# The even attentions' subtraction reads the spread maxima from SBUF, copied there by ScalarE

## Chip, core and metric

One Trainium2 chip, one of its cores. The metric is the device time of one execution in microseconds. Engines are named as in the profile: PE is TensorE, DVE is VectorE, ACT is ScalarE, POOL is GpSimd. All data is 32-bit float.

## The reference, cut to what matters

The network has two blocks of a first model and one of a second. Only the first layer (the "even" one) is touched: two attentions over 1024 latent tokens and 256 context tokens, 8 query heads and 2 key heads of width 64. Attention A lets every latent query see all 1280 keys; attention B sees a band of three 128-key tiles, the context, and one extra "sink" logit.

```python
def gqa_attend(q, k, v, bias=None, sink=None):
    s = jnp.einsum("bqhgd,bkhd->bhgqk", q, k) * ATTN_SCALE
    if bias is not None:
        s = s + bias
    ...
        p = jax.nn.softmax(s, axis=-1)
    return jnp.einsum("bhgqk,bkhd->bqhgd", p, v)
```

The softmax is computed with a maximum that is subtracted before the exponential. The sum of the exponentials divides the result at the end.

## The kernel before

Scores are held transposed: 128 keys on the partitions, and 8 heads x 128 queries along a row, so one **item** is one key tile of one query tile, 128x1024 numbers. A **group** is one query tile with all its key tiles: in A eight groups of 10 items and two context groups of 2 (84 items), in B groups of 4 or 5 and two of 2 (42 items). The functions `soft_attention` of PE, ACT and DVE and `prob_sums` of POOL run A, then B; between them the projections of B are computed, and nothing else overlaps them.

`group_plan` writes the order out by hand as steps, one item per step. Every engine goes through the same steps in program order, so an engine that waits holds back all its later work:

- F, "fill": PE computes the scores of item n into one of two PSUM buffers (L1056), and ACT copies them into an SBUF ring (L1569). DVE keeps a running maximum over the items of the group, reading the PSUM scores and the SBUF maximum (L2046, `maximum`).
- M0, M1, R0, R1: after the group's last item PE transposes the maximum (L1043) and DVE reduces it over the keys, negated (L2072); in B the sink is taken in (L2079, L2080), which are two instructions on 8 columns.
- NB: PE spreads the 8 negated maxima over 128 partitions and 1024 columns with 8 transposes into two PSUM banks, `NM_BC` (L1068).
- B: three steps after the group's last fill and later, one item per step: DVE adds `NM_BC` to the item in the ring (L2029, `subtract`), ACT takes the exponential in place (L1578), POOL adds the item to the group's running sum of probabilities (L650; none for the first item of a group, as the second add takes both), and two steps later PE multiplies with the values (L1089).
- OE, DEN, RC, MIX, OM: at the end of the group the output is gated (L2053), PE turns the sums into denominators (L1108), DVE takes reciprocals (L2065 in A, L2063 in B), PE spreads them (L1100), and DVE multiplies them in (L2087).

The ring has 17 items in A and 12 in B; a fill waits until the item that lay in its place has been multiplied and added. DVE's order in a step is: closing work of an older group, `subtract`, `maximum`; only in the NB step does the maximum go first. ACT's order is fill, then exponential. PE's NB waits until the negated maxima are ready and until DVE has subtracted the last item of the group before, since `NM_BC` has one copy:

```python
pe.wait_ge(at["neg_max"], g + 1)
if g:
    pe.wait_ge(at["shifted"], first[g])
```

Of the kernel before, what the change touches and what calls it, by code (L numbers as in the profile page):

```python
# [6 lines left out]
ACT = mybir.ActivationFunctionType  # L7
# [3 lines left out]
P = 128  # L11
# [120 lines left out]
def program(nc, wall, wdown, wglr, wgate2, vec, xl_in, xc_in, consts, ropes, bmask, dmask, rpb, out):  # L132
    with ExitStack() as ctx:
# [248 lines left out]

        scale_q = DH ** -0.5

        MASK_PREV, MASK_NEXT = area(SCR + 6656, P), area(SCR + 6656 + P, P)
        LOW = [XL[:, k, :] for k in range(KT)] + [area(SCR + 1024 * i, 1024) for i in range(6)]
        HIGH = [area(22016 + 4 * TOK + 1024 * i, 1024) for i in range(5)]
        XC_LOW, XC_HIGH = XC[:, 0:1024], XC[:, 1024:2048]
# [14 lines left out]
        for name, groups, ring, g_rows in (("A", [group_a(*x) for x in lat_ctx], LOW + HIGH, 0),  # L403
                                           ("B", [group_b(*x) for x in lat_ctx], LOW, 4)):
            items, first, plan = group_plan([len(gr["keys"]) for gr in groups])
            at = {"groups": groups, "items": items, "first": first, "plan": plan, "ring": ring[:-2], "sums": [XC_HIGH, ring[-1]],
                  "maxes": [XC_LOW, ring[-2]], "g_rows": g_rows,
                  "sink": name == "B"}
            for x in ("st", "filled", "masked", "maxed", "max_t", "reduced", "neg_max", "bcast", "shifted", "exped", "pooled",
                      "pv", "o_out", "den", "recip", "r_bcast", "mixed") + (("sink_in", "sink_out") if name == "B" else ()):  # L410
                at[x] = sem(f"att{name}_{x}")
            at["is_masked"] = [groups[g]["keys"][j][1] is not None for g, j in items]
            at["max_before"] = [first[g] - g for g in range(len(groups) + 1)]
            at["misc"] = []
            for st in plan:
                for half in range(2):
                    at["misc"] += [("MT", st[f"M{half}"], half)] if f"M{half}" in st else []
                at["misc"] += [("MIX", st["MIX"], 0)] if "MIX" in st else []
                at["misc"] += [("DEN", st["DEN"], 0)] if "DEN" in st else []
            soft[name] = at  # L420
# [349 lines left out]
        def _(pe):  # L770
# [258 lines left out]
            def soft_attention(at, t_next):  # L1029
# [31 lines left out]
                for st, ahead in zip(at["plan"], at["plan"][1:] + [{}]):  # L1061
                    if "NB" in st:
                        g = st["NB"]
                        pe.wait_ge(at["neg_max"], g + 1)
                        if g:
                            pe.wait_ge(at["shifted"], first[g])
                        for h in range(HEADS):
                            mm = pe.transpose(ps[:, NM_BC + h * P:NM_BC + (h + 1) * P],  # L1068
                                              ST[:, g % 4, 1, h:h + 1].to_broadcast([P, P]), IDENT)
                        mm.then_inc(at["bcast"], 1)  # L1070
                    if "F" in ahead:
                        fill(ahead["F"])
                    for half in range(2):
                        if f"M{half}" in st:
                            max_transposes(st[f"M{half}"], half)
                    if "PV" in st:
                        n = st["PV"]
                        g, j = items[n]
                        kt = groups[g]["keys"][j][0]
                        pe.wait_ge(at["exped"], n + 1)  # L1080
                        if j == 0 and g:
                            pe.wait_ge(at["o_out"], g)
                        p = ring[n % len(ring)]
                        for kv in range(2):
                            for half in range(2):
                                r = slice(64 * half, 64 * half + 64)
                                o = PV_O + 256 * kv
                                heads = p[:, kv * BANK:(kv + 1) * BANK].rearrange("p (x a q) -> p x a q", x=2, a=2)[:, :, half, :]
                                mm = pe.matmul(ps[r, o:o + 256], VE[:, kt, 64 * kv:64 * kv + 64], heads,  # L1089
                                               start=(j == 0 and kv == 0), stop=(j == len(groups[g]["keys"]) - 1),  # L1090
                                               skip_group_check=True)
                        mm.then_inc(at["pv"], 1)
                    if "MIX" in st:
                        g = st["MIX"]
                        pe.wait_ge(at["recip"], g + 1)
                        misc_wait("MIX", g, 0)
                        for x in range(4):
                            for half in range(2):
                                h = 2 * x + half
                                mm = pe.matmul(ps[64 * half:64 * half + 64, MISC + x * P:MISC + (x + 1) * P],  # L1100
                                               ST[:, g % 4, 2, h:h + 1].to_broadcast([P, 64]), IDENT, start=True, stop=True)
                        mm.then_inc(at["r_bcast"], 1)
                    if "DEN" in st:
                        g = st["DEN"]
                        pe.wait_ge(at["pooled"], at["max_before"][g + 1])
                        misc_wait("DEN", g, 0)
                        for h in range(HEADS):
                            mm = pe.matmul(ps[:, MISC + 2 * h:MISC + 2 * h + 2], at["sums"][g % 2][:, h * P:(h + 1) * P], ONES[:, 0:2],  # L1108
                                           start=True, stop=True)
                        mm.then_inc(at["den"], 1)  # L1110
# [329 lines left out]
        def _(act):  # L1440
# [115 lines left out]
            def soft_attention(at):  # L1556
                ring, items = at["ring"], at["items"]
                for st in at["plan"]:
                    if "F" in st:
                        n = st["F"]  # L1560
                        if at["is_masked"][n]:
                            act.wait_ge(at["masked"], sum(at["is_masked"][:n + 1]))
                        else:
                            act.wait_ge(at["st"], n + 1)
                        if n >= len(ring):
                            act.wait_ge(at["pv"], n - len(ring) + 1)
                            act.wait_ge(at["pooled"], pooled_upto(at, n - len(ring)))
                        o = S_T + 2 * (n % 2) * BANK
                        act.activation(ring[n % len(ring)], ps[:, o:o + 2 * BANK], ACT.Copy).then_inc(at["filled"], 1)  # L1569
                    if at["sink"] and "NB" in st:  # L1570
                        g = st["NB"]
                        act.wait_ge(at["sink_in"], g + 1)
# [180 lines left out]
        def _(dve):  # L1753
# [264 lines left out]
            def soft_attention(at):  # L2018
# [5 lines left out]
                def subtract(n):  # L2024
                    g, j = items[n]
                    if j == 0:
                        dve.wait_ge(at["bcast"], g + 1)
                    p = ring[n % len(ring)]
                    dve.tensor_tensor(p, ps[:, NM_BC:NM_BC + 1024], p, ALU.add).then_inc(at["shifted"], 1)  # L2029

                def maximum(n):
                    g, j = items[n]
# [455 lines left out]
```

## Time and profile before

| | us |
|---|---|
| median of 3 runs | 3201.89 (3201.58 to 3202.61) |
| the profiled execution, its own time | 3198.09 |
| its span in the trace | 3196.3 |
| PE busy | 3028.5 (95%) |
| DVE busy | 1480.0 (46%) |
| ACT busy | 761.3 (24%) |
| POOL busy | 596.5 (19%) |
| POOL's adds of probabilities, L650, 106 of them | 251.0 |
| DVE's subtractions, L2029, 126 of them | 151.4 |

The busy shares are those of the whole program, most of which is matrix products; what counts here are the two attentions, from 247.8 us (the first ACT fill) to about 530 us, and from about 712 us to about 916 us. POOL works in them far more than its 19% says. The last two rows are sums of the groups of the page by line.

### The profile page before, as it was taken

What the parts mean: (1) busy time and instruction counts of PE and PEld (TensorE: products, weight loads), DVE (VectorE), ACT (ScalarE), POOL (GpSimd) and SP (SyncE); (2) the same over time, 40 slices, a digit from 0 to 9 for tenths busy, and PEclk for the clock granted to TensorE, in tenths of its full rate; (3) what the DMA queues carried; (4) which work ended last, traced back from release to release, by engine and by line L of the source; (5) the groups of instructions that cost most, each with busy time, mean ns of one, the idle gap of its engine ahead of it and who ended that gap; (6) DMA issues with size and microseconds to landing.
All of it is one profiled execution on the core that took longest, in us unless ns stands there. A gap on an engine that the chain in (4) does not pass through costs nothing.

```text
span 3196.3 us, 27666 instructions
## 1 busy us (share of the span) xinstructions
PE 3028.5 (95%) x11326; PEld 1554.0 (49%) x11326; DVE 1480.0 (46%) x1858; ACT 761.3 (24%) x923; POOL 596.5 (19%) x394
## 2 busy tenths in 40 slices
PE   7998898997889999999999999999999999999997
PEld 4563445653455545444774545454444444444443
DVE  4636873248846586735773311035453343340001
ACT  4116662005410210113641122122012222220000
POOL 0004673003410122233441000000112222210000
PEclk9999998999889899999999899999999999999998
DMA  6001000020033211123221001100211111112101
GB/s 222 27 27 40 1 1 7 27 87 1 1 121 110 112 40 40 40 68 80 55 91 45 30 20 40 33 27 20 92 40 43 50 40 41 52 50 89 36 36 53
DMA packets 41071, 162.42 MB, mean 51 GB/s; under 512 B 5265, under 2 KB 5777, under 8 KB 36721
## 3 DMA queue, kind: packets, MB, share of 16 engines
q1 hardware_dynamic: 34704, 143.18, 12.8%
q0 software_dynamic: 6240, 17.47, 2.2%
q8 instruction: 90, 1.47, 0.2%
q14 instruction: 37, 0.30, 0.0%
HBM read 148.04 MB, written 15.20 MB: 51 GB/s over the span
## 4 chain that ended last, share of the span: by engine, by line
PE 86%; DVE 7%; ACT 3%; issue 2%; POOL 1%; DMA 1%; SPq 0%; DVEq 0%; ACTq 0%; POOLq 0%
PE ps L794 28%; PE ps L787 20%; PE ps L1433 9%; PE ps L1319 4%; PE ps L1272 3%; PE ps L1206 2%; PE ps L1056 2%; PE ps L969 2%; PE ps L1089 2%; PE ps L984 2%; PE ps L998 2%; PE ps L1108 1%; PE ps L902 1%; DVE x_ctx L2046 1%; DVE arena L2046 1%
## 5 line engine op out<-in xcount | busy, mean ns | idle before, releaser
L787 PE MATMUL ps<-arena 128*128 128x512 f32 (+1 forms) x1632 | 625.6, 544 | 15.8 <-ACT arena L1485 10.9
L787 PEld LDWEIGHTS ps<-arena 128*128 128x128 f32 x1632 | 311.5, 192 | 321.0 <-issue 306.8
L794 PE MATMUL ps<-arena 128*128 128x512 f32 x936 | 411.3, 592 | 3.2 <-DVE arena L2248 1.6
L794 PE MATMUL ps<-x_lat,arena 128*128 128x512 f32 x688 | 303.9, 592 | 0.0
L794 PEld LDWEIGHTS ps<-arena 128*128 128x128 f32 x936 | 177.6, 190 | 227.2 <-issue 223.8
L1433 PE MATMUL ps<-arena 128*128 128x512 f32 x616 | 264.5, 592 | 0.0
L794 PEld LDWEIGHTS ps<-x_lat,arena 128*128 128x128 f32 x688 | 130.7, 190 | 164.5 <-issue 164.5
L1056 PE MATMUL ps<-arena 64*128 64x512 f32 x504 | 152.7, 687 | 49.6 <-DVE x_ctx L2046 23.8
L1433 PEld LDWEIGHTS ps<-arena 128*128 128x128 f32 x616 | 117.0, 190 | 147.3 <-issue 147.3
L2223 DVE SCALAR_TENSOR_TENSOR x_ctx<-arena,vectors,x_ctx 128x1024 f32<-128x1024 f32 x120 | 169.6, 1413 | 3.5
L1468 ACT ACTIVATE arena<-x_lat 128x1024 f32<-128x1024 f32 x40 | 42.0, 1050 | 465.7 <-DVEq L2177 343.3
L794 PE MATMUL ps<-x_lat,x_ctx 128*128 128x512 f32 x336 | 147.6, 592 | 0.0
L2169 DVE TENSOR_TENSOR x_lat<-ps,x_lat 128x1024 f32<-128x1024 f32 x10 | 12.2, 1224 | 279.1 <-PE ps L1433 279.0
L1319 PE MATMUL ps<-arena 128*128 128x512 f32 x256 | 123.7, 606 | 0.0
L2383 DVE TENSOR_TENSOR x_ctx<-ps,x_ctx 128x512 f32<-128x512 f32 x21 | 14.5, 692 | 225.9 <-ACT x_ctx L1742 225.9
L725 POOL TENSOR_TENSOR arena<-arena 128x512 f32<-128x512 f32 x6 | 10.8, 1793 | 580.3 <-DMA arena<-in_wall 449.1
L794 PEld LDWEIGHTS ps<-x_lat,x_ctx 128*128 128x128 f32 x336 | 63.8, 190 | 80.4 <-issue 80.4
L1056 PEld LDWEIGHTS ps<-arena 64*128 64x128 f32 x504 | 40.7, 196 | 104.2 <-DVE x_ctx L2046 43.3
L1906 DVE SCALAR_TENSOR_TENSOR arena<-arena,silu_c 128x128 f32<-128x128 f32 (+1 forms) x224 | 89.9, 479 | 0.0
L1578 ACT ACTIVATE x_lat<-x_lat 128x1024 f32<-128x1024 f32 x70 | 73.8, 1055 | 65.4 <-DVE x_lat L2029 64.5
L1272 PE MATMUL ps<-arena 128*128 128x512 f32 x192 | 85.4, 604 | 1.8 <-DMA arena<-in_wall 1.8
L2029 DVE TENSOR_TENSOR x_lat<-ps,x_lat 128x1024 f32<-128x1024 f32 x70 | 84.2, 1212 | 2.4 <-PE ps L1068 2.1
(284 smaller groups left out, 4137.3 us busy)
## 6 DMA issues: line engine op xcount, KB each, us to landing
arena<-in_wall SPq DMA_DIRECT2D x188, 512.0 KB, 3.8
arena<-in_wdown SPq DMA_DIRECT2D x7, 1408.0 KB, 6.0
x_lat<-in_xl_in SPq DMA_DIRECT2D x8, 1024.0 KB, 9.5
residual_store<-x_lat SPq DMA_DIRECT2D x8, 1024.0 KB, 6.8
x_lat<-residual_store SPq DMA_DIRECT2D x8, 1024.0 KB, 8.6
x_lat<-expanded_bias POOLq DMA_DIRECT2D x48, 160.0 KB, 3.6
arena<-expanded_bias POOLq DMA_DIRECT2D x32, 160.0 KB, 4.0
out<-x_lat SPq DMA_DIRECT2D x8, 512.0 KB, 3.0
```

The source lines that it names most:

```text
L787: mm = pe.matmul(ps[:, o + c:o + c + n], W[:, ring_of(g) % WSLOTS, k, :], rhs(k, c, n), start=(k == 0), stop=(k == KT - 1))
L794: mm = pe.matmul(ps[:, bank * BANK:(bank + 1) * BANK], weights[:, k, :], tokens[:, k, :], start=(start and k == 0), stop=(k == 3), skip_gr ...
L969: mm = pe.matmul(ps[:, o:o + n], DQ[r, j, qt * P:(qt + 1) * P], DK[r, j, k0:k0 + n], start=True, stop=True)
L984: mm = pe.transpose(ps[:, o:o + P], DP[u % 3][:, a, i * P:(i + 1) * P], IDENT)
L1056: mm = pe.matmul(ps[:, o:o + BANK], QK[r, 4, kt * P:(kt + 1) * P], QK[r, 0:4, c0:c1], start=True, stop=True)
L1272: mm = pe.matmul(ps[:, o:o + 512], HG[:, k, i * P:(i + 1) * P], W[:, :, k, :], start=(k == 0), stop=(k == KT - 1))
L1319: mm = pe.matmul(ps[:, R_PS + c:R_PS + c + n], W[:, (g0 + 16 + m) % WSLOTS, k, :], HG[:, k, c:c + n], start=(k == 0), stop=(k == KT - 1))
L1433: mm = pe.matmul(ps[:, o + c:o + c + n], wd[:, k, :], ACTV[:, k, c:c + n], start=(k == 0), stop=(k == DOWN_K - 1))
L1578: act.activation(p, p, ACT.Exp).then_inc(at["exped"], 1)
L1906: ins = dve.scalar_tensor_tensor(t, x, SC[:, k, a:a + 1], t, ALU.mult, ALU.add)
L2029: dve.tensor_tensor(p, ps[:, NM_BC:NM_BC + 1024], p, ALU.add).then_inc(at["shifted"], 1)
L2223: link(dve.scalar_tensor_tensor(acc, U[:, j, k:k + LAT], V[:, w + k:w + k + 1], acc, ALU.mult, ALU.add))
```

## The change

The 8 transposes of NB still go to PSUM. Then ACT copies the two banks into a new SBUF tile `NMS` of 1024 columns, and DVE's subtraction reads `NMS` where it read PSUM. There are 20 such copies, one for each group. PE's next NB waits for the copy (`spread`) and no longer for the last subtraction; the copy takes over that wait, because `NMS` has one copy too. The two 128-column masks of B move 512 columns up to make room.

```diff
-        MASK_PREV, MASK_NEXT = area(SCR + 6656, P), area(SCR + 6656 + P, P)
+        NMS = area(SCR + 6 * 1024, 1024)
+        MASK_PREV, MASK_NEXT = area(SCR + 7 * 1024, P), area(SCR + 7 * 1024 + P, P)
...
                         pe.wait_ge(at["neg_max"], g + 1)
                         if g:
-                            pe.wait_ge(at["shifted"], first[g])
+                            pe.wait_ge(at["spread"], g)
...
                         act.activation(ring[n % len(ring)], ps[:, o:o + 2 * BANK], ACT.Copy).then_inc(at["filled"], 1)
+                    if "NB" in st:
+                        g = st["NB"]
+                        act.wait_ge(at["bcast"], g + 1)
+                        if g:
+                            act.wait_ge(at["shifted"], at["first"][g])
+                        act.activation(NMS, ps[:, NM_BC:NM_BC + 1024], ACT.Copy).then_inc(at["spread"], 1)
...
                     if j == 0:
-                        dve.wait_ge(at["bcast"], g + 1)
+                        dve.wait_ge(at["spread"], g + 1)
                     p = ring[n % len(ring)]
-                    dve.tensor_tensor(p, ps[:, NM_BC:NM_BC + 1024], p, ALU.add).then_inc(at["shifted"], 1)
+                    dve.tensor_tensor(p, NMS, p, ALU.add).then_inc(at["shifted"], 1)
```

On ACT, in attention A, around the NB step of the fifth group, the order before is (L1569 the fill, L1578 the exponential):

```order
L1569 ACTIVATE x_lat<-ps 128x1024 [waits attA_pooled,attA_pv,attA_st]
L1578 ACTIVATE x_lat<-x_lat 128x1024 [waits attA_shifted]
L1569 ACTIVATE x_lat<-ps 128x1024 [waits attA_pooled,attA_pv,attA_st]
L1578 ACTIVATE x_lat<-x_lat 128x1024 [waits attA_shifted]
L1569 ACTIVATE x_lat<-ps 128x1024 [waits attA_pooled,attA_pv,attA_st]
```

and in the changed kernel, at the same place (L1570 the fill, L1576 the copy, L1585 the exponential):

```order
L1570 ACTIVATE x_lat<-ps 128x1024 [waits attA_pooled,attA_pv,attA_st]
L1585 ACTIVATE x_lat<-x_lat 128x1024 [waits attA_shifted]
L1570 ACTIVATE x_lat<-ps 128x1024 [waits attA_pooled,attA_pv,attA_st]
L1576 ACTIVATE arena<-ps 128x1024 [waits attA_shifted,attA_bcast]
L1585 ACTIVATE x_lat<-x_lat 128x1024 [waits attA_shifted]
L1570 ACTIVATE x_lat<-ps 128x1024 [waits attA_pooled,attA_pv,attA_st]
```

The copy stands between the fill and the exponential of the NB step. On DVE, around the NB step of the second group of A, the order before is (L2029 the subtraction, L2046 the maximum, L2053 the gating of OE):

```order
L2029 TENSOR_TENSOR arena<-ps,arena 128x1024
L2046 TENSOR_TENSOR x_ctx<-ps,x_ctx 128x1024 [waits attA_maxed,attA_filled] x2
L2029 TENSOR_TENSOR arena<-ps,arena 128x1024 [waits attA_bcast]
L2029 TENSOR_TENSOR arena<-ps,arena 128x1024
L2046 TENSOR_TENSOR x_ctx<-ps,x_ctx 128x1024 [waits attA_maxed,attA_filled]
L2053 TENSOR_TENSOR arena<-ps,arena 128x4x128 [waits attA_pv]
```

and in the changed kernel, where the three are L2036, L2053 and L2060:

```order
L2036 TENSOR_TENSOR arena<-arena 128x1024
L2053 TENSOR_TENSOR x_ctx<-ps,x_ctx 128x1024 [waits attA_maxed,attA_filled] x2
L2036 TENSOR_TENSOR arena<-arena 128x1024 [waits attA_spread]
L2036 TENSOR_TENSOR arena<-arena 128x1024
L2053 TENSOR_TENSOR x_ctx<-ps,x_ctx 128x1024 [waits attA_maxed,attA_filled]
L2060 TENSOR_TENSOR arena<-ps,arena 128x4x128 [waits attA_pv]
```

No instruction of DVE moves. Both inputs of the subtraction are now in SBUF (`arena`), and the first one of a group waits for the copy in place of the transposes.

## Rows read from the trace of the kernel before

**Rows 1.** Stages: span; PE, PEld, DVE, ACT, POOL busy (instructions); PE clock; DMA.

```profile
272.00:504.00 232.00, 206.39 (x1300) 98.43 (x1300) 189.86 (x187) 151.05 (x154) 171.19 (x72) 0.95 0.05 12
504.00:529.00 25.00, 18.86 (x112) 15.89 (x112) 4.05 (x9) 1.33 (x2) 7.62 (x4) 0.58 0.00 1
734.00:893.00 159.00, 131.33 (x824) 70.43 (x820) 131.76 (x145) 75.50 (x86) 73.13 (x31) 0.90 0.00 1
```

**Rows 2.** Groups by line and form: busy us, mean ns, idle before.

```profile
L2029 DVE TENSOR_TENSOR arena<-ps,arena 128x1024 f32<-128x1024 f32 x56 | 67.2, 1211 | 2.7 <-PE ps L1068 2.5
L1920 DVE TENSOR_TENSOR arena<-arena 128x1024 f32<-128x1024 f32 x10 | 12.3, 1226 | 0.3
L650 POOL TENSOR_TENSOR arena<-arena,x_lat 128x1024 f32<-128x1024 f32 x31 | 73.3, 2363 | 35.4 <-ACT x_lat L1578 33.1
```

**Rows 3.** What L1068, the spreading transposes, waited for: us, times.

```profile
  DVE x_lat L2029: 4.3, 4
  DVE arena L2029: 2.2, 3
```

**Rows 4.** Timeline of DVE in another stage: start us, us, engine, line.

```profile
1107.51 2.29 DVE L1795 TENSOR_TENSOR x_lat<-arena,x_lat 128x2048 f32<-128x2048 f32 x1
1109.84 3.24 DVE L1797 TENSOR_TENSOR x_lat<-arena,x_lat 128x2048 f32<-128x2048 f32 x1
1113.01 3.35 DVE L1798 TENSOR_TENSOR x_lat<-arena 128x2048 f32<-128x2048 f32 x1
```

**Rows 5.** Timeline of POOL in the same stretch.

```profile
1107.87 3.06 POOL L702 TENSOR_TENSOR arena<-arena 128x512 f32<-128x512 f32 x1 [190.08 <-DMA arena<-in_wall]
1110.90 3.31 POOL L703 TENSOR_TENSOR arena<-arena 128x512 f32<-128x512 f32 x1
...
1117.56 1.26 POOL L709 TENSOR_TENSOR arena<-arena 128x512 f32<-128x512 f32 x1
```

**Rows 6.** L2079 in B: duration ns min/median/max, first and last start; then one timeline row.

```profile
L2079 DVE TENSOR_TENSOR softmax_stats<-softmax_stats,negated_sink x10: 166/1970/2173, 729.5 to 878.1; 128x8 f32<-128x8 f32 x10
...
781.93 2.17 DVE L2079 TENSOR_TENSOR softmax_stats<-softmax_stats,negated_sink 128x8 f32<-128x8 f32 x1
```

**Rows 7.** Timeline of POOL at that place.

```profile
781.73 2.34 POOL L650 TENSOR_TENSOR x_ctx<-x_ctx,x_lat 128x1024 f32<-128x1024 f32 x1
```

**Rows 8.** Timeline of DVE in a middle group of attention A.

```profile
360.50 2.34 DVE L2029 TENSOR_TENSOR arena<-ps,arena 128x1024 f32<-128x1024 f32 x2
...
367.75 1.21 DVE L2029 TENSOR_TENSOR arena<-ps,arena 128x1024 f32<-128x1024 f32 x1
...
370.02 1.21 DVE L2029 TENSOR_TENSOR x_lat<-ps,x_lat 128x1024 f32<-128x1024 f32 x1
...
376.34 1.23 DVE L2046 TENSOR_TENSOR x_ctx<-ps,x_ctx 128x1024 f32<-128x1024 f32 x1 [0.51 <-ACT arena L1569]
379.24 0.69 DVE L2087 TENSOR_TENSOR arena<-ps,arena 128x512 f32<-128x512 f32 x1 [1.68 <-PE ps L1100]
```

**Rows 9.** Timeline of POOL in the same group.

```profile
358.50 2.38 POOL L650 TENSOR_TENSOR x_ctx<-x_ctx,arena 128x1024 f32<-128x1024 f32 x1 [0.23 <-ACT arena L1578]
...
367.87 2.37 POOL L650 TENSOR_TENSOR arena<-arena 128x1024 f32<-128x1024 f32 x1 [0.77 <-ACT arena L1578]
```

**Rows 10.** Timeline of ACT at that group's NB step.

```profile
358.32 1.00 ACT L1569 ACTIVATE arena<-ps 128x1024 f32<-128x1024 f32 x1
```

**Rows 11.** The chain that ended last, at the end of attention A.

```profile
487.15 2.37 POOL arena L650
...
504.72 2.35 POOL arena L650
...
507.12 2.87 PE ps L1108 x16
```

**Rows 12.** Timeline of DVE at the end of attention A.

```profile
486.62 3.48 DVE L2029 TENSOR_TENSOR x_lat<-ps,x_lat 128x1024 f32<-128x1024 f32 x3
...
501.96 2.36 DVE L2029 TENSOR_TENSOR arena<-ps,arena 128x1024 f32<-128x1024 f32 x2 [0.64 <-PE ps L1068]
```

More of the change, by code:

```diff
@@ L408, in program @@
                   "sink": name == "B"}
-            for x in ("st", "filled", "masked", "maxed", "max_t", "reduced", "neg_max", "bcast", "shifted", "exped", "pooled",
+            for x in ("st", "filled", "masked", "maxed", "max_t", "reduced", "neg_max", "bcast", "spread", "shifted", "exped", "pooled",
                       "pv", "o_out", "den", "recip", "r_bcast", "mixed") + (("sink_in", "sink_out") if name == "B" else ()):
```

## The prediction

> **What bounds the kernel now.** I read the page first and then the busy times by stage, since the change touches only the two attentions. The page says that PE is 95% busy, but that is the whole program. In attention A, the first row of [rows 1], PE is busy 206 of 232 us, DVE 190, POOL 171, ACT 151, for 84 items, or 2.76 us an item. No engine is far from the bound, and all walk through the same steps in order, so what delays one delays the rest soon after. In B, its third row, DVE is busy 132 of 159 us and POOL only 73. Nothing runs beside the attentions that could fill a gap, so time lost there is time of the kernel. In the steady middle of a group of A the beat is set by DVE: two subtractions start at 367.75 and 370.02, 2.27 us apart [rows 8], which is one subtraction and one maximum with no idle between. POOL's adds last 2.36 us each [rows 2], nine to a group of ten items, and lie beside DVE's work without touching it: the subtraction with one PSUM input has a mean of 1.21 us [rows 2], though an add runs beside most of them.
>
> **What is removed.** PE's wait for the last subtraction before it spreads the next maxima. The transposes waited for it 7 times, 6.5 us in all [rows 3]. The copy takes over that wait, so where PE waited before, ACT waits now and then copies. A fill of the same size out of PSUM takes 1.00 us [rows 10]; the 8 transposes, which now run ahead of the wait, took about as long. That is an exchange, and I count nothing for it; at best 6.5 us come back.
>
> **What is added: 20 copies on ACT.** 20 x 1.00 = 20 us of ACT. At the NB step the copy stands behind the fill. The fill of [rows 10] ends at 359.32; DVE then does the maximum over it, and begins the first subtraction at 360.50 [rows 8]. A copy from 359.32 to 360.32 is ready 0.2 us before that. The exponential behind it waits for that subtraction anyway. So the copy is covered by the maximum: 0 us; if that cover is gone everywhere, 20 us. I take 0, as the one place is typical of all groups that still have fills, and the last groups have the exchange above.
>
> **What is moved: the subtraction's first input, from PSUM to SBUF.** Its own length does not change by much. DVE's addition of two SBUF inputs, L1920, has 1.226 us against 1.211 us for L2029 [rows 2]: 126 x 0.015 = 2 us, within the rest. The page "VectorE: DVE Perf Modes" of the Trainium skill, in its section on the SBUF-source errata, gives 58 cycles of fixed cost from SBUF and 120 from PSUM at 0.96 GHz, which would make it an estimated 8 us gain; the two rows here show no such difference.
>
> But with both inputs in SBUF, DVE's instruction and POOL's add are no longer independent. The trace shows it elsewhere. At 1107.51 DVE begins an addition of two SBUF inputs, which lasts its 2.29 us [rows 4]. POOL's addition begins at 1107.87 and takes 3.06 us [rows 5], where the same shape alone takes 1.26 (its last row). It ends at 1110.93, 1.13 us after DVE's end. The next of DVE began at 1109.84 and takes 3.24 us, 0.95 more than the first: it ends at 1113.08, 2.15 us after POOL's end. POOL's next, in turn, takes 3.31. They go strictly one after the other, each waiting for the whole of the other. The same thing is seen with the very add of this stage: in B the 8-column L2079, two SBUF inputs, takes 0.17 us at the least and 2.17 at the most, 1.97 in the middle [rows 6]. The one at 781.93 ends at 784.10, just after the add that ran from 781.73 to 784.07 [rows 7]. So the hold is not a matter of size, and L2029 escaped it only through its PSUM input. This is the decisive row.
>
> From those rows the holds are: DVE 2.15 us for 2048 columns, so 1.08 for 1024; POOL 1.13 for an addition that lasts 1.26, 0.13 less, so 2.36 - 0.13 = 2.23 for ours. The page "SBUF — State Buffer" of the Trainium skill, section "Who interferes with whom", states the rule: a VectorE instruction with two SBUF inputs and a GpSimd one that reads SBUF share a read interface, which the first holds for its whole instruction. It speaks against this change, and the trace agrees. With whole instructions as holds (1.22 and 2.36) in place of those measured from end to end, the lower bound below would be 84 x 1.22 + 72 x 2.36 - 232 = 40 us and not 20.
>
> **The lower bound.** From 272 to 504 us A has 84 subtractions and 72 adds [rows 1]. In turn they need 84 x 1.08 + 72 x 2.23 = 251 us, 19 more than the 232 there are. Only if neither ever left the other an unused moment would it stay at that: +19.
>
> **The upper bound.** A beat of subtraction, add, subtraction is 1.08 + 2.23 = 3.31 us where it was 2.27, so 1.04 more for each add, 74 in A: +77. In B, POOL is busy 73 of 159 us, 46%; 42 subtractions that fall in at random would wait 42 x 0.46 x 2.23 / 2 = 22 us. Together +99.
>
> **What I take.** I walk through a middle group of A. Its first subtraction at 360.50 would meet the add that began at 358.50 and ended at 360.88 [rows 8, 9]; as that add has itself been held up by the subtraction before, the wait is nearer 1.3 us than 0.4. In the steady part each subtraction starts inside an add: that of 370.02 inside the add of 367.87, which ends at 370.24 [rows 8, 9]; once POOL is behind, it waits for most of one, 1.04 per item. Of the group's other eight items some two stand where the subtractions are over 3 us apart, with reductions between them, so six count: 6.2 us. Against it, DVE has 0.51 + 1.68 = 2.2 us of idle at the group's end, waiting for PE [rows 8], which is then late no more. 1.3 + 6.2 - 2.2 = 5.3, say 5 us a group, and seven groups up to 487 us: 35 us.
>
> At the end of A the chain is POOL itself: eight adds back to back from 487.15 to 507.07, and PE's denominators wait for the last of them [rows 11]. Ten subtractions start in that time, the first as one of the three from 486.62 on, the last as one of the two from 501.96 [rows 12]. Each now takes its turn: 10 x 1.08 = 11 us, say 10 of them on the chain.
>
> In B, L2079 already waits out the running add just before the late subtractions, and L2079's own wait only grows by what POOL has been pushed. I take 8 us, between 0 and 22, nearer the lower end because POOL idles over half of B.
>
> Sum: 35 + 10 + 8 = 53 us. What is late next is PE: with more idle time its granted clock may fall. It is 0.95 in A, 0.90 in B and 0.58 in the thin end of A [rows 1]; full level is 2.4 GHz and the lower one 1.2. I put nothing into the sum for it, and some into the range. The profiled execution took 3198.1 us, so 3251 by its own time; the median of the runs is 3.8 us above it, so 3255.
>
> **The rivals.**
> 1. *The add and the subtraction do not exclude each other.* Then only the removed wait and the 2 us of the longer form count: between 3201.9 - 6.5 = 3195 and 3204. For it: the subtraction waits nowhere now. Against it: [rows 4 to 6], with half of the ten L2079 at 1.97 us or more. It would have to be that a PSUM-free subtraction is exempt. 6%, half of it faster by more than the 0.2%, about 6 us, that a measurement of this kernel can tell from no change.
> 2. *They do, but the waits hide,* because the order of the two settles so that a subtraction falls into POOL's pauses. A pause exists: POOL idles 61 of the 232 us of A. But the bound of 19 us is made without any loss, so this gives 3202 + 19 = 3221, slower all the same: 15%, in 3216 to 3230.
> 3. *ACT's copy is uncovered.* When DVE waits for POOL the copy has more time, not less, so it would take an NB step at which the fill comes late and no maximum follows. +20 on top of the forecast: 3275. 5%.
> 4. *PE's clock decides.* If A fell from 0.95 to the 0.81 or less of a stretch like its end, 206 us of PE work would become 206 x 0.95 / 0.81 = 242, +36, of which half may hide behind DVE's and POOL's waits: 3255 + 18 = 3273, and with the upper bound 3301 and more. 9%, half of it above 3300.
>
> **How the numbers follow.** The forecast, 3230 to 3300 around 3255, has 65%; rival 2 15%, rival 3 5%, rival 4 9%, rival 1 6%. The range 3216 to 3300 leaves out rival 1 and half of rival 4 and a rest at both edges, some 15% together. Faster by over 0.2%: 3%. Within 0.2%: 4%, the other half of rival 1 and a bound that was too high. Slower: 93%.
>
> **What the changed profile would show.** In A the subtraction's mean rises from 1.21 to about 1.8 us and more, with a spread from 1.2 to 3.4; the add's mean rises from 2.36 to about 3 us. The steady beat of subtractions becomes 3.3 us. The stage from 272 to 504 grows by 35 to 45 us; B's by under 20. The maximum L2046, which keeps a PSUM input, stays at 1.22 us, and projections, the odd layer and the second model keep their times. I am wrong if the subtraction keeps 1.22 us while POOL adds; the size is wrong if the adds' mean grows but the stage does not, which would mean PE set the pace after all.

## The result, and the profile after

The changed kernel takes 3253.3 us (median of 4 runs, 3251.3 to 3256.6), the kernel before 3201.7 beside it (4 runs). The ratio is 1.016, 95% interval 1.015 to 1.018: some 52 us slower. The profiled execution took 3251.3 us, its span is 3249.5.

The busy times by stage, first of the kernel before, then of the changed one. The stages are cut at the first ACT fill and the last multiplication (L2087, now L2094) of each attention: attention A, the projections between, attention B, the rest. The columns are those of [rows 1].

```profile
247.80:529.20 281.40, 242.79 (x1484) 119.92 (x1480) 209.80 (x208) 167.66 (x169) 178.80 (x75) 0.92 0.04 11
529.20:716.50 187.30, 183.43 (x630) 108.41 (x632) 61.53 (x167) 12.44 (x11) 0.00 (x0) 0.97 0.14 46
716.50:917.50 201.00, 159.88 (x980) 89.67 (x976) 148.77 (x168) 85.42 (x95) 75.47 (x32) 0.86 0.02 6
917.50:3196.30 2278.80, 2218.07 (x7330) 1103.96 (x7330) 946.40 (x1247) 438.83 (x579) 342.03 (x283) 0.98 0.17 56
```

```profile
249.00:583.20 334.20, 259.32 (x1484) 125.94 (x1481) 286.08 (x208) 176.91 (x179) 224.63 (x75) 0.87 0.03 9
583.20:767.20 184.00, 180.04 (x630) 105.51 (x632) 61.71 (x168) 12.45 (x11) 0.00 (x0) 0.99 0.14 47
767.20:966.90 199.70, 154.83 (x980) 86.22 (x976) 150.34 (x168) 94.54 (x105) 79.48 (x32) 0.89 0.02 6
966.90:3249.50 2282.60, 2221.58 (x7330) 1106.73 (x7330) 946.87 (x1246) 439.11 (x579) 341.41 (x283) 0.98 0.17 56
```

Attention A grew by 52.8 us. B did not grow at all: -1.3. The other two stages moved by -3.3 and +3.8, with the same instructions in them; by so much a stage can move with nothing changed in it. In A DVE is busy for 76 us more (same 208 instructions) and POOL for 46 us more (same 75). An instruction that waits inside the engine counts as busy, so the wait shows as duration. The subtraction and the add in the changed kernel, answering to [rows 2]:

```profile
L2036 DVE TENSOR_TENSOR x_lat<-arena,x_lat 128x1024 f32<-128x1024 f32 x70 | 131.2, 1884 | 3.4 <-ACT arena L1576 3.2
L2036 DVE TENSOR_TENSOR arena<-arena 128x1024 f32<-128x1024 f32 x56 | 111.4, 2000 | 7.3 <-ACT arena L1576 7.2
L651 POOL TENSOR_TENSOR arena<-arena,x_lat 128x1024 f32<-128x1024 f32 x31 | 89.6, 2890 | 28.1 <-ACT x_lat L1585 24.9
```

The subtraction's mean is 1.93 us (131.2 + 111.4 = 242.6 us for 126) where it was 1.21; the add's, in the form shown, 2.89 where it was 2.36. The steady part of a group, DVE's timeline in the changed kernel, answering to [rows 8], with subtraction L2036 and maximum L2053:

```profile
286.24 2.25 DVE L2036 TENSOR_TENSOR x_lat<-arena,x_lat 128x1024 f32<-128x1024 f32 x1
288.42 1.21 DVE L2053 TENSOR_TENSOR arena<-ps,arena 128x1024 f32<-128x1024 f32 x1
289.55 2.26 DVE L2036 TENSOR_TENSOR x_lat<-arena,x_lat 128x1024 f32<-128x1024 f32 x1
291.73 1.21 DVE L2053 TENSOR_TENSOR arena<-ps,arena 128x1024 f32<-128x1024 f32 x1
292.87 2.25 DVE L2036 TENSOR_TENSOR x_lat<-arena,x_lat 128x1024 f32<-128x1024 f32 x1
```

and POOL's timeline there:

```profile
284.09 9.94 POOL L651 TENSOR_TENSOR x_ctx<-x_ctx,x_lat 128x1024 f32<-128x1024 f32 x3 [2.26 <-ACT x_lat L1585]
```

The subtractions start every 3.31 us, three adds take 9.94, also 3.31 each; the maximum with its PSUM input still takes 1.21. That is the beat of the prediction to the hundredth: 1.08 + 2.23.

### The profile page after: what moved, and what is told of

It reads as the page before. It is cut to its first block, busy times and chain, and to the rows that moved or that the text cites. A ratio compares the mean times of both kernels' runs of the same rounds, so it can differ in the third digit from the quotient of the medians.

```text
span 3249.5 us, 27704 instructions
## 1 busy us (share of the span) xinstructions
PE 3041.5 (94%) x11326; PEld 1556.9 (48%) x11326; DVE 1558.6 (48%) x1858; ACT 780.0 (24%) x943; POOL 645.7 (20%) x394
## 4 chain that ended last, share of the span: by engine, by line
PE 81%; DVE 11%; issue 3%; ACT 3%; DMA 1%; POOL 0%; SPq 0%; DVEq 0%; ACTq 0%
PE ps L795 28%; PE ps L788 19%; PE ps L1434 9%; PE ps L1320 3%; PE ps L1273 3%; DVE x_lat L2036 2%; DVE arena L2036 2%; PE ps L1207 2%; PE ps L970 2%; PE ps L985 2%; DVE arena L2053 2%; PE ps L999 2%; DVE x_ctx L2053 1%; PE ps L819 1%; PE ps L903 1%
## 5 line engine op out<-in xcount | busy, mean ns | idle before, releaser
L795 PE MATMUL ps<-arena 128*128 128x512 f32 x936 | 411.3, 592 | 3.2 <-DVE arena L2255 1.6
L1434 PE MATMUL ps<-arena 128*128 128x512 f32 x616 | 264.5, 592 | 0.0
L2176 DVE TENSOR_TENSOR x_lat<-ps,x_lat 128x1024 f32<-128x1024 f32 x10 | 12.2, 1224 | 279.1 <-PE ps L1434 279.0
L2036 DVE TENSOR_TENSOR x_lat<-arena,x_lat 128x1024 f32<-128x1024 f32 x70 | 131.2, 1884 | 3.4 <-ACT arena L1576 3.2
L1320 PE MATMUL ps<-arena 128*128 128x512 f32 x256 | 123.8, 606 | 0.0
L2036 DVE TENSOR_TENSOR arena<-arena 128x1024 f32<-128x1024 f32 x56 | 111.4, 2000 | 7.3 <-ACT arena L1576 7.2
L1585 ACT ACTIVATE x_lat<-x_lat 128x1024 f32<-128x1024 f32 x70 | 73.9, 1056 | 89.8 <-DVE x_lat L2036 89.5
L651 POOL TENSOR_TENSOR arena<-arena,x_lat 128x1024 f32<-128x1024 f32 x31 | 89.6, 2890 | 28.1 <-ACT x_lat L1585 24.9
```

The costliest lines, as they stand in the source:

```text
L651: pool.tensor_tensor(total, one, ring[n % len(ring)], ALU.add).then_inc(at["pooled"], 1)
L795: mm = pe.matmul(ps[:, bank * BANK:(bank + 1) * BANK], weights[:, k, :], tokens[:, k, :], start=(start and k == 0), stop=(k == 3), skip_gr ...
L1320: mm = pe.matmul(ps[:, R_PS + c:R_PS + c + n], W[:, (g0 + 16 + m) % WSLOTS, k, :], HG[:, k, c:c + n], start=(k == 0), stop=(k == KT - 1))
L1434: mm = pe.matmul(ps[:, o + c:o + c + n], wd[:, k, :], ACTV[:, k, c:c + n], start=(k == 0), stop=(k == DOWN_K - 1))
L1585: act.activation(p, p, ACT.Exp).then_inc(at["exped"], 1)
L2036: dve.tensor_tensor(p, NMS, p, ALU.add).then_inc(at["shifted"], 1)
```

## The experiments

Each kernel ran beside the kernel before on the same chip; before had 3199.4 us there in four of the experiments (copy kept, inputs swapped, and the two without POOL's reading; 15 runs) and, on another chip, 3200.4 in the next four (half the add, B alone, the sink's minimum, the changed kernel again; 21 runs). The last two experiments ran once each, beside one run of the kernel before (3197.5).

**The copy without the new operand.** Only the subtraction's source is put back.

```diff
-                    dve.tensor_tensor(p, NMS, p, ALU.add).then_inc(at["shifted"], 1)
+                    dve.tensor_tensor(p, ps[:, NM_BC:NM_BC + 1024], p, ALU.add).then_inc(at["shifted"], 1)
...
                             pe.wait_ge(at["spread"], g)
+                            pe.wait_ge(at["shifted"], first[g])
```

> The changed kernel with one part undone: ACT still makes the 20 copies and DVE still waits for them, but the subtraction reads the spread maxima from PSUM again; PE waits for both the copy and the last subtraction. Theory (DVE's subtraction with two SBUF inputs and POOL's add exclude each other): the subtraction's mean is back at 1.21 us and the add's at 2.36, and the time at 3202, within 4 us. Rival (the copy and its waits on ACT cost the time): the time stays near 3253 and the subtraction's mean is irrelevant.

Measured: 3199.8 us (10 runs), ratio 1.0003, interval 0.9994 to 1.0013. The subtraction is back at 1.21 us, as the rows by line say (duration ns min/median/max, first and last start):

```profile
L2037 DVE TENSOR_TENSOR x_lat<-ps,x_lat x70: 1169/1214/1225, 272.1 to 888.7; 128x1024 f32<-128x1024 f32 x70
L2037 DVE TENSOR_TENSOR arena<-ps,arena x56: 1169/1214/1225, 292.4 to 870.4; 128x1024 f32<-128x1024 f32 x56
```

So the 20 copies, 20 us of ACT, and their waits cost nothing that can be measured as long as the subtraction reads PSUM, and the loss hangs on one operand of the subtraction.

**The inputs in the other order.**

```diff
-                    dve.tensor_tensor(p, NMS, p, ALU.add).then_inc(at["shifted"], 1)
+                    dve.tensor_tensor(p, p, NMS, ALU.add).then_inc(at["shifted"], 1)
```

> The changed kernel with the subtraction's two inputs in the other order (item first, spread maxima second). Theory (any two SBUF inputs exclude POOL's add): 3253 within 3 us, the subtraction's mean again near 1.94 us. Rival (only the tensor in the second place counts, or the two reads of the new 1024 columns conflict with something): the time moves by more than 10 us.

Measured: a median of 3261.9 us, with the profiled execution at 3250.2 and the three others from 3260.2 to 3267.8. In the profiled execution the subtractions are those of the changed kernel (medians 1.53 and 2.15 us, against 1.53 and 2.14), so the order plays no part in the exclusion. The median lies 9 us above the 3253 expected. To see whether that is the order's doing, the changed kernel was run again:

> The changed kernel once more, to stand beside e2_inputs_swapped, whose profiled run had 3250.2 us as the changed kernel's 3251.3, but whose timed runs lay at 3260 to 3268. If those were a drift of TensorE's granted clock on that chip (0.956 to 0.960 in them, 0.963 in the profiled run), this kernel too shows runs between 3250 and 3268. If the order of inputs costs 8 us, it stays at 3251 to 3257.

Measured: 3252.0, 3255.9, 3263.0 and 3261.4 us, at a mean PE clock of 0.962, 0.962, 0.957 and 0.959. The changed kernel spreads in the same way, and its long runs too have the lower clock. As it ran on another chip, the medians (1.019 and 1.018 of the kernel before) show only that no cost of the order can be told from this spread. The change's cost was 52 us in the first comparison and is 58 in this one. Whether the lower clock makes the long runs long, or goes with something else that does, these times do not show.

**POOL's reading taken away.** In the changed kernel and in the one before, the add becomes a fill, which takes 0.95 us.

```diff
-                    pool.tensor_tensor(total, one, ring[n % len(ring)], ALU.add).then_inc(at["pooled"], 1)
+                    pool.memset(total, 1.0).then_inc(at["pooled"], 1)
```

> The changed kernel with POOL's add of probabilities replaced by a fill of the running sum with ones, which reads nothing from SBUF; the sums of probabilities, and so the division, are left out of the computation. Theory (POOL's reading excludes DVE's two-input instruction): every subtraction takes 1.22 us, the 8-column minimum of attention B 0.17, and the time equals that of the kernel before with the same replacement, or is up to 6.5 us below it. Rival (the cost sits in the longer reading of SBUF, or in POOL's writing): the time stays some 50 us above the kernel before with the same replacement.

> The kernel before with POOL's add replaced by the same fill with ones (the sums of probabilities are left out). Theory: the 8-column minimum of attention B no longer waits (0.17 us each, 1.7 in all, where it was 16.1 us), and POOL no longer sets the end of attention A (eight adds in a row, 20 us, against ten subtractions): 3202 - 14 for the minimum - about 5 at the end of A = 3183, between 3175 and 3195. Rival (POOL costs nothing in the kernel before, as its subtraction has only one SBUF input): 3202 within 4 us.

Measured: 3185.7 us (ratio to before 0.9962, 0.9949 to 0.9975) and 3186.0 us (0.9960, 0.9945 to 0.9974), five runs each. Without reads by POOL the two kernels are equal; the change's own effect, less the exclusion, is nothing. The changed kernel's subtraction and 8-column minimum:

```profile
L2036 DVE TENSOR_TENSOR x_lat<-arena,x_lat x70: 1170/1214/1226, 273.8 to 878.7; 128x1024 f32<-128x1024 f32 x70
...
L2086 DVE TENSOR_TENSOR softmax_stats<-softmax_stats,negated_sink x10: 166/167/168, 726.3 to 866.3; 128x8 f32<-128x8 f32 x10
```

Every one of them has its plain duration. The fill also writes 1024 columns of SBUF, so it is POOL's reading, or the length of its instruction, and not its writing that holds DVE up; the length is settled by the next experiment, where an add of 1.26 us, hardly longer than the fill of 0.95, still takes turns with the subtraction. The kernel before gained 13 us by the same edit, where 14 + 5 = 19 were expected, though inside the expected range. In its profiled execution B is 12.1 us shorter (188.9, where it was 201.0), and A as a whole 2.0 (279.4, where it was 281.4), not the 5 expected of its end.

**Half the add.** POOL adds 512 columns of each item.

```diff
-                    pool.tensor_tensor(total, one, ring[n % len(ring)], ALU.add).then_inc(at["pooled"], 1)
+                    pool.tensor_tensor(total[:, 0:512], one[:, 0:512], ring[n % len(ring)][:, 0:512], ALU.add).then_inc(at["pooled"], 1)
```

> The changed kernel with POOL adding only 512 of the 1024 columns of each item (the sums of the last four heads are left out; PE takes the first four heads' twice). Theory (exclusion with holds in proportion to the instruction): the add holds 1.13 us, so subtraction, add, subtraction needs 1.08 + 1.13 = 2.21 us, below the 2.27 of DVE's own beat; the steady beat returns to 2.27 to 2.5 and the time falls to 3190 to 3205. Rival (every meeting costs a fixed time, whatever the add's length): some 50 us stay, 3235 or more.

Measured: 3203.8 us (11 runs), ratio 1.0010, 1.0001 to 1.0019, inside the range expected. The instructions still exclude each other: DVE's timeline there, and POOL's,

```profile
286.26 1.21 DVE L2036 TENSOR_TENSOR x_lat<-arena,x_lat 128x1024 f32<-128x1024 f32 x1
287.39 1.21 DVE L2053 TENSOR_TENSOR arena<-ps,arena 128x1024 f32<-128x1024 f32 x1
288.52 1.21 DVE L2036 TENSOR_TENSOR x_lat<-arena,x_lat 128x1024 f32<-128x1024 f32 x1
```

```profile
281.94 13.70 POOL L651 TENSOR_TENSOR x_ctx<-x_ctx,x_lat 128x512 f32<-128x512 f32 x6
```

The beat is 2.26 us again, and six adds of 1.26 us take 13.7, that is 2.28 each: POOL waits out every subtraction and fits into the time of the maximum. In the steady part, then, what costs is not the meeting but the sum of the two holds being longer than DVE's own beat.

That the whole time is back at that of the kernel before is partly a coincidence. Attention A and attention B of this run:

```profile
249.80:541.30 291.50, 249.19 (x1484) 122.70 (x1480) 221.73 (x208) 176.64 (x179) 132.72 (x75) 0.90 0.04 10
726.20:917.50 191.30, 155.67 (x980) 88.64 (x977) 136.48 (x168) 95.12 (x105) 44.08 (x32) 0.87 0.02 7
```

A still takes 10 us more than before (291.5, where it was 281.4) and 12 more than with POOL's reading gone (279.5); B takes 10 less, as the adds there are halved too and the sink's minimum hardly waits (0.42 us in the middle, where it was 1.97). So half the add removes some 43 of A's 53 us. Of the 10 us that stay, 8 lie behind A's sixth closing multiplication (67.3 us, where it was 59.4). There subtractions follow each other without a maximum between, and three in a row take 6.1 us, where they took 3.5. The kernel before with half the adds was not run.

**The new operand in B alone.** A reads PSUM as before, B reads the copy.

```diff
-                    dve.tensor_tensor(p, NMS, p, ALU.add).then_inc(at["shifted"], 1)
+                    dve.tensor_tensor(p, NMS if at["sink"] else ps[:, NM_BC:NM_BC + 1024], p, ALU.add).then_inc(at["shifted"], 1)
...
                             pe.wait_ge(at["spread"], g)
+                            if not at["sink"]:
+                                pe.wait_ge(at["shifted"], first[g])
```

> The changed kernel with attention A's subtraction reading PSUM again (its copies stay), so that only B's 42 subtractions read SBUF. The changed kernel's trace shows B as long as before, 199.7 us where it was 201.0, since the 8-column minimum lost 11 of the 16 us that it waited while the subtractions gained 13. Theory (the waits in B only change their place): 3197 to 3202, no difference from the kernel before that can be measured. Rival (B's share is the 8 us of the prediction): 3207.

Measured: 3201.5 us (11 runs), ratio 1.0001, 0.9992 to 1.0010. With the new operand in B alone nothing is lost that can be measured, so the 52 us are A's. The rows of B say why, two of this kernel by line (busy us, mean ns), against a minimum of 16.1 us in ten and subtractions of 1.21 us in the kernel before:

```profile
L2038 DVE TENSOR_TENSOR x_lat<-arena,x_lat 128x1024 f32<-128x1024 f32 x30 | 46.8, 1568 | 3.2 <-ACT arena L1578 3.2
...
L2088 DVE TENSOR_TENSOR softmax_stats<-softmax_stats,negated_sink 128x8 f32<-128x8 f32 x10 | 3.3, 328 | 0.3
```

**The sink's minimum out of POOL's way.** This is the kernel before, without the change. The reduction writes its 4 columns to PSUM, and what follows has one input there.

```diff
+                        if at["sink"]:
+                            c = slice(4 * half, 4 * half + 4)
+                            top = ps[:, MISC:MISC + 4]
+                            link(dve.tensor_reduce(top, ps[:, MISC:MISC + BANK].rearrange("p (h k) -> p h k", h=4), AX_X, ALU.max,
+                                                   negate=True))
+                            link(dve.tensor_tensor(nm[:, c], top, NSINK[:, c], ALU.min))
+                            if half == 1:
+                                dve.engine_nop().then_inc(at["neg_max"], 1)
+                            link(dve.tensor_tensor(top, top, vcol("sink", 4 * half, 4), ALU.add))
+                            ins = dve.tensor_scalar(ST[:, g % 4, 3, c], top, 0.0, None, ALU.min)
...
```

> The kernel before, with the sink's part in attention B in another form: the reduction writes its 4 columns to PSUM, and the minimum with the negated sink, and the sum with it, take that PSUM input and one SBUF input, half by half; two more reductions' worth of small instructions for each group, each about 0.2 us with its link. Theory (DVE's instructions with at most one SBUF input never wait for POOL): no small instruction lasts over 0.2 us, where L2079 lasted 16.1 us in ten; against it stand some 0.8 us more of small instructions in each of ten groups: 16 - 1.7 - 8 = 6 us faster, 3193. Rival (the small instructions wait for something else, or the group's pace is set elsewhere): 3199 or slower.

Measured: 3190.9 us (5 runs), ratio 0.9969, 0.9956 to 0.9981: 6 to 14 us faster than the kernel before, the fastest full kernel of this study. Its small instructions, by line:

```profile
L2080 DVE TENSOR_TENSOR ps<-ps,vectors 128x4 f32<-128x4 f32 x20 | 3.4, 169 | 0.8
L2077 DVE TENSOR_TENSOR softmax_stats<-ps,negated_sink 128x4 f32<-128x4 f32 x20 | 3.2, 162 | 0.7
L2081 DVE TENSOR_SCALAR softmax_stats<-ps 128x4 f32<-128x4 f32 x20 | 3.2, 162 | 0.7
```

9.8 us of sixty instructions stand where 16.1 + 1.7 us of twenty stood, and the longest of the sixty takes 0.17 us. Attention B is 195.0 us there, against 201.0; A, in which nothing was changed, is 2.4 us shorter in the same execution, so the 6 us of B are known to some 2 us only:

```profile
710.90:905.90 195.00, 157.13 (x980) 88.41 (x977) 140.73 (x208) 86.31 (x95) 75.56 (x32) 0.87 0.02 6
```

**The long one at the start.** In the changed kernel one subtraction, the third of A, lasts 5.2 us, more than any add. DVE's and POOL's timelines there:

```profile
277.70 5.22 DVE L2036 TENSOR_TENSOR x_lat<-arena,x_lat 128x1024 f32<-128x1024 f32 x1
```

```profile
275.93 3.43 POOL L635 DMA_DIRECT2D expanded_bias<-in_rpb  x1 [275.49 <-ACT x_lat L1585]
279.36 2.47 POOL L651 TENSOR_TENSOR x_ctx<-x_lat 128x1024 f32<-128x1024 f32 x1
```

It starts 1.66 us before the add does, and yet ends behind it, at 282.92. It is no accident of one execution: with the inputs swapped, and in the second trace of the changed kernel, it takes 5.21 us. Two kernels, one run each:

```diff
-            pool.dma_start(expanded.rearrange("h r q k -> (h r) q k"), src).then_inc(table_in, 16)
...
             prob_sums(soft["A"])
+            pool.dma_start(expanded.rearrange("h r q k -> (h r) q k"), src).then_inc(table_in, 16)
```

> The changed kernel with POOL's one DMA at the start of attention A (the expanded bias table, 3.4 us of descriptors on POOL) issued after A's adds. In the changed kernel the third subtraction of A begins at 277.70 us inside that issue and lasts 5.2 us, through the issue and the whole add behind it. Theory (it waits because of what POOL does there): the third subtraction lasts at most 2.3 us, and attention A from its first fill to its last multiplication is 2 to 4 us shorter than 334.2. Rival (the long one has another cause): it stays at about 5 us.

```diff
             pool.dma_start(expanded.rearrange("h r q k -> (h r) q k"), src).then_inc(table_in, 16)
+            pool.wait_ge(soft["A"]["exped"], 2)
+            pool.memset(XC_HIGH[:, 0:8], 0.0).then_inc(u_zero, 1)
+            pool.wait_ge(u_zero, 1)
```

> The changed kernel with a fill of 8 columns, which reads nothing, between that DMA and the first add, and a wait of POOL for it. With POOL's add replaced by a fill (e3) the third subtraction lasted 1.2 us beside the same DMA issue. Theory (an add that stands ready behind the issue takes the shared read side before it starts): the third subtraction lasts at most 2.3 us. Rival (it is the issue itself that is held together with an add somewhere behind it): it lasts about 5 us.

Measured, with the DMA moved away: the third subtraction lasts 3.34 us, above the 2.3 that I had written, since it met the add at its very start and waited for all of it (2.23 + 1.08 = 3.31). With the fill between, DVE's and POOL's timelines:

```profile
278.82 1.22 DVE L2039 TENSOR_TENSOR x_lat<-arena,x_lat 128x1024 f32<-128x1024 f32 x1
```

```profile
277.05 3.43 POOL L635 DMA_DIRECT2D expanded_bias<-in_rpb  x1 [276.61 <-ACT x_lat L1588]
280.37 0.23 POOL L637 MEMSET x_ctx<- 128x8 f32 x1
280.68 2.35 POOL L654 TENSOR_TENSOR x_ctx<-x_lat 128x1024 f32<-128x1024 f32 x1
```

Beside the same DMA issue the third subtraction takes its plain 1.22 us. So the issue itself does not hold it; an add that stands ready behind the issue does, before its own record begins. A as a whole hardly gained: from the first fill to the last multiplication 333.5 and 334.1 us, against 334.2, less than the 2 to 4 expected of the first. Up to the first closing multiplication they were 2.5 and 2.8 us shorter; they lost it again in the five groups behind it (173.3 and 174.1 us, against 171.5), at a PE clock of 0.86 in A, where the changed kernel had 0.87.

The two executions took 3260.7 and 3262.7 us, as long as the longest of the changed kernel, and their traces are the only ones of such an execution. The extra is in B, which has the same instructions as in the changed kernel. The first of the two:

```profile
765.90:974.30 208.40, 163.68 (x980) 91.65 (x976) 150.83 (x168) 94.78 (x105) 79.53 (x32) 0.84 0.02 6
```

B takes 208.4 us in both, where the changed kernel had 199.7, at a PE clock of 0.84 and 0.83 against 0.89, with DVE busy as long as there. Why is open.

## Why the prediction was right, and where it was not

**The mechanism** was right, and so was its price. The exclusion was read from [rows 4 to 7], and the beat of 3.31 us from their ends. The first and third experiments leave no other cause: put the operand back, or take POOL's reading away, and the loss is gone. The signs named came true as well: the subtraction's mean is 1.93 us, its longest 3.37 apart from the one of 5.2, and the maximum stays at 1.21 to 1.23.

**The copy at nothing** was right for the copies alone, with which the time did not move. In the groups that still have fills their cover was as described. At the end of A and B, where no maximum follows, DVE waits 10.4 us for them in the changed kernel (3.2 + 7.2 in the rows by line above), where PE waited 6.5 us for DVE [rows 3] and DVE in turn some 5 us for PE: the exchange that was counted at nothing. At the end of A it is not quite nothing once DVE is behind: two of these waits lie on the chain shown further down.

**The longer form of the instruction**: a median of 1.21 us with either source once POOL's reads are gone. The estimated 8 us gain from the page "VectorE: DVE Perf Modes" of the Trainium skill, section on the SBUF-source errata, did not come: without the exclusion the two kernels stand at 3185.7 and 3186.0.

**Attention A: 45 us forecast, 52.8 measured.** The rows of the first and sixth closing multiplication, before

```profile
319.94 0.69 DVE L2087 TENSOR_TENSOR arena<-ps,arena 128x512 f32<-128x512 f32 x1 [2.56 <-PE ps L1100]
469.79 0.69 DVE L2087 TENSOR_TENSOR arena<-ps,arena 128x512 f32<-128x512 f32 x1 [2.77 <-PE ps L1100]
```

and after,

```profile
331.18 0.69 DVE L2094 TENSOR_TENSOR arena<-ps,arena 128x512 f32<-128x512 f32 x1 [0.54 <-PE ps L1101]
502.70 0.68 DVE L2094 TENSOR_TENSOR arena<-ps,arena 128x512 f32<-128x512 f32 x1
```

give 149.9 and 171.5 us for five middle groups, 4.3 us more for each; 5 was forecast. The waits for PE of 2.6 to 2.8 us ahead of the multiplication, which the walk let absorb 2.2 us a group, are indeed down to 0.5 and none. From A's first fill to the first of these rows A lost 10.0 us where 5 were counted. The 5.2 us subtraction lies there, 4 us over its plain length; with the DMA moved away this stretch took 79.6 us and with the fill between 79.3, where it was 82.2, so it accounts for half of the 5 us that were not counted. Where the other half lies was not tried. The larger miss is the end: from 469.79 to the last multiplication A took 59.4 us before and 80.5 after, 21 us more, where the forecast had one group and the end, 15. The failed step there is "the chain is POOL itself": the eight adds took 26.0 us where they had taken 19.9, 6 us more and not the 10 counted, but they no longer end last. The chain is now DVE's, and then the copies':

```profile
524.48 3.52 DVE x_lat L2036 x2
...
528.90 3.37 DVE x_lat L2036
...
532.39 3.17 DVE arena L2036
...
536.16 9.29 DVE arena L2036 x3
...
546.44 1.02 ACT arena L1576
...
547.48 4.56 DVE arena L2036 x2
...
553.03 1.01 ACT arena L1576
...
554.07 3.75 DVE arena L2036 x2
```

Where [rows 11] have eight adds back to back, the five subtractions from 528.90 on each start inside an add with no maximum before them to use the time, and last 3.1 to 3.4 us. The walk put ten subtraction holds on POOL's chain, and left out that DVE, too, loses the whole add each time. Behind them come the last two groups, each of which must wait for the exponential of the group before and for its copy: 2.0 us twice, half of it the copy (1.02 and 1.01). From the end of the eighth add, at 550.95, PE's denominators come 9.6 us later, where they followed in 0.05 us before.

**Attention B: +8 forecast, -1.3 measured.** The step that failed is "L2079's own wait only grows by what POOL has been pushed". The subtractions of B did gain 13.4 us (42 of them, 64.0 where 50.6 stood), between the 8 taken and the 22 of the upper bound. But the minimum, L2079 and now L2086, fell from 16.1 us to 4.9. In [rows 6, 7] it started 0.20 us inside the second add of its group and waited it out. In the changed kernel that add, pushed back by a subtraction, starts 0.20 us behind the minimum, and the next subtraction meets it instead (two lines of DVE, one of POOL):

```profile
835.07 0.17 DVE L2086 TENSOR_TENSOR softmax_stats<-softmax_stats,negated_sink 128x8 f32<-128x8 f32 x1
836.50 2.24 DVE L2036 TENSOR_TENSOR x_lat<-arena,x_lat 128x1024 f32<-128x1024 f32 x1
```

```profile
835.27 2.38 POOL L651 TENSOR_TENSOR x_ctx<-x_ctx,x_lat 128x1024 f32<-128x1024 f32 x1
```

So pushing POOL did not lengthen that wait but moved it to another instruction, where it is paid once. In two of the ten groups the minimum still waits, 1.8 us each. How firmly B stands at nothing depends on the execution: 199.7 us here, but 208.4 in the two long ones above.

**PE's clock**, left out of the sum: 0.92 in A before and 0.87 after, and back at 0.93 with the operand put back or POOL's reading gone, so it fell because of the exclusion; what it adds to the 52.8 us was not separated. The 0.81 of rival 4 is in none of the rows shown, where the end of A has 0.58. The runs of the changed kernel spread from 3251 to 3263. That belongs in the range, where it was. The two misses, +8 in A and -9 in B, cancel. That 3255 came so near to 3253 is luck, which the steps did not earn.

**A misread row**: the 72 instructions of POOL in the first of [rows 1] are 71 adds and the DMA issue, so the lower bound was 17 us and not 19. Rival 2, which was built on it, becomes 3219 in place of 3221; nothing else changes.

**"They exclude each other, but the waits hide"** came true for B. With half the add it came true in the steady part of A, where the two holds, 1.08 + 1.13, fit into DVE's beat of 2.27, but not where there is no maximum between subtractions: 10 us stayed.

## What to carry to other kernels

Before an operand of a VectorE instruction is moved from PSUM to SBUF, look at what GpSimd reads meanwhile: with one PSUM input the two run side by side, with two SBUF inputs they take turns, each for nearly its whole length (1.08 of 1.21 us, 2.23 of 2.36). Add up the two holds and compare them with the beat of the stage: above it the difference is paid at every item; below it the steady part is free (2.21 against 2.27 here), but not a stretch in which such instructions follow each other directly. Then follow the chain at the stage's end anew, as another engine may come last there. And look for small instructions with odd maxima (0.17 us at the least, 2.17 at the most): they show such an exclusion already at work, and giving them a PSUM input made this kernel 0.3% faster.

## What the runs showed of the hardware that was not expected

- POOL can hold back DVE before its add is recorded as started: with the add ready behind a DMA issue, DVE's two-input instruction waited from 277.70 us, 1.66 us before the add's start, and lasted 5.2 us in three traces. With an 8-column fill between issue and add it did not wait at all (one trace). How long ahead an add takes hold in general, the runs do not show.
- A fill of 1024 columns by POOL (0.95 us) leaves DVE's two-input instruction at 1.21 us. The page "SBUF — State Buffer" of the Trainium skill, section "Who interferes with whom", says that such an instruction contends with a GpSimd instruction that reads SBUF and not with one that only writes it; the trace agrees, in 126 subtractions.
- The hold goes with the length of the instruction, not with its being there: by [rows 4, 5] 1.13 us for 512 columns, and 2.23 for 1024, which with DVE's 1.08 is the measured beat of 3.31.
- The same kernel took 3252 to 3263 us on one chip, with PE's mean clock from 0.962 down to 0.957. Two traces of nearly the same kernel at 0.958 have the extra in attention B: 208.4 us at a clock of 0.84 and 0.83 there, against 199.7 at 0.89.
